# MLP up projection of a transformer block in seven half-size products in place of eight, for six of its eight chunks

## The reference, cut to what matters

```python
D_MODEL = 1024; SEQ = 1024; D_FF = 4 * D_MODEL     # one layer, batch 1, float32

def squared_relu_mlp(h, w1, w2):
    a = jax.nn.relu(h @ w1)
    return (a * a) @ w2
...
        x = x + g1 * (mix_lat @ w_out[i])
        x = x + g2 * squared_relu_mlp(modulate(x, g_mlp[i], sh2, sc2), w_mlp1[i], w_mlp2[i])
```

## Time and profile before

| | |
|---|---|
| median of 3 runs | 1398.17 us (1398.11 to 1398.28) |
| profiled execution, span from first to last instruction | 1394.5 us (the page gives no other time of that execution) |
| PE busy | 1351.0 us, 97% |
| DVE / ACT / POOL busy | 66% / 50% / 35% |
| MLP part of the span | about 730 us to the end |
| granted PE clock, mean | 0.994 |
| DMA | 143.42 MB, mean 103 GB/s |

### The profile page before, as it was taken

One profiled execution on the slowest core, in us unless ns is written; L12 is line 12 of the kernel. 1 busy time (PEld: TensorE's weight loads), 2 busy tenths in 40 slices (PEclk: granted clock), 3 DMA queues, 4 the chain that ended last, 5 costly groups with the idle time before them and its releaser, 6 DMA issues.

```text
span 1394.5 us, 18825 instructions
## 1 busy us (share of the span) xinstructions
PE 1351.0 (97%) x7262; PEld 1144.5 (82%) x7262; DVE 914.7 (66%) x1284; ACT 692.6 (50%) x1343; POOL 487.0 (35%) x321
## 2 busy tenths in 40 slices
...
GB/s 376 189 172 161 173 159 290 125 90 86 128 197 141 183 131 192 71 1 61 37 71 121 32 30 91 31 76 31 69 40 27 91 31 76 31 64 44 15 61 121
DMA packets 121576, 143.42 MB, mean 103 GB/s; under 512 B 8184, under 2 KB 103288, under 8 KB 118672
## 3 DMA queue, kind: packets, MB, share of 16 engines
q1 hardware_dynamic: 121232, 142.18, 32.3%
...
q0 software_dynamic: 256, 0.05, 0.0%
...
## 4 chain that ended last, share of the span: by engine, by line
PE 77%; DVE 12%; ACT 6%; DMA 2%; issue 1%; POOL 1%; SPq 0%; DVEq 0%; ACTq 0%
PE f_ps L2065 24%; PE f_ps L2334 19%; PE a_ps L1425 7%; PE o_ps L1773 6%; PE a_ps L1441 5%; PE a_ps L1471 5%; PE f_ps L2350 3%; ACT s_pr L1522 3%; DVE s_nmx L1607 2%; PE t_ps L956 2%; DMA t_wm<-in_w_mod 1%; PE t_ps L945 1%; PE t_ps L971 1%; ACT l_pr L1539 1%; DVE l_nb L1612 1%
## 5 line engine op out<-in xcount | busy, mean ns | idle before, releaser
L2065 PE MATMUL f_ps<-h,f_w 128*128 128x512 f32 x1536 | 358.0, 389 | 0.4 <-DVE h L1839 0.3
L2065 PEld LDWEIGHTS f_ps<-h,f_w 128*128 128x128 f32 x1536 | 288.2, 188 | 60.6 <-DVE h L1839 0.7
L2264 DVE TENSOR_TENSOR mix<-mix,f_ps 128x512 f32<-128x512 f32 x196 | 128.8, 684 | 152.8 <-PE f_ps L2334 152.8
L2105 POOL TENSOR_TENSOR f_w<-f_w,f_g 128x1024 f32<-128x1024 f32 x30 | 77.1, 2592 | 389.9 <-DMA f_w<-in_w_mlp 342.5
L2142 ACT ACTIVATE f_a<-f_ps 128x512 f32<-128x512 f32 x64 | 38.2, 597 | 255.0 <-PE f_ps L2065 254.9
L2334 PE MATMUL f_ps<-f_bl,f_ah 128*128 128x512 f32 x392 | 152.6, 389 | 0.0
L2334 PE MATMUL f_ps<-f_bh,f_ah 128*128 128x512 f32 x392 | 152.6, 389 | 0.0
L2334 PE MATMUL f_ps<-f_bh,f_al 128*128 128x512 f32 x392 | 152.5, 389 | 0.0
L1621 DVE TENSOR_TENSOR l_pT<-a_ps,l_pT 128x512 fp32r<-128x512 f32 (+1 forms) x192 | 109.0, 594 | 53.0 <-ACT l_pT L1532 53.0
L1425 PE MATMUL a_ps<-l_k,l_q 96*128 96x512 f32 (+1 forms) x576 | 136.4, 366 | 0.5 <-DVE l_mo L1633 0.5
L956 PE MATMUL t_ps<-w_in,t_h 128*128 128x416 f32 (+2 forms) x600 | 123.4, 351 | 0.3 <-DVE w_in L719 0.3
...
## 6 DMA issues: line engine op xcount, KB each, us to landing
...
f_w1r<-in_w_mlp SPq DMA_DIRECT2D x32, 512.0 KB, 4.1
f_w<-in_w_mlp SPq DMA_DIRECT2D x16, 1024.0 KB, 5.0
t_wm<-in_w_mod SPq DMA_DIRECT2D x8, 1024.0 KB, 12.6
...
```

What stands on the lines that cost most here:

```text
L2065: last = nc.tensor.matmul(ps[:, b, :], w1[:, g % 2, w, k, :], h2[x][:, k, half * HB:(half + 1) * HB], start=(k == 0 and i == 0), stop=(k = ...
L2264: V.tensor_tensor(x, x, ps[:, bank_of(i, t), :].rearrange("p (k c) -> p k c", c=P), ALU.add).then_inc(added, 1)
```

## The change

In chunks 2 to 7 the up projection too is made of seven half-size products, P5, P3, P2, P1, P6, P7, P4 in this order. h is cut in four quarters (token half `th`, half `kh` of the 1024 inputs), the chunk's part of w1 likewise ("11" to "22": input half, half of the 512 columns). Each product is 2 hidden tiles x 4 k x 3 = 24 matmuls of 512 tokens: 7 x 24 = 168 a chunk where there were 192. The results are chained in PSUM and through `a`: P5, P3 and P2 are copied out by ACT (`copy`), P1, P6 and P7 are added by DVE onto such a copy (`add`), ReLU and square follow (`square`).

- P2, P1 and P4 take quarters of `h2` as they are. P5, P3, P6 and P7 need four sums of quarters of h. They are made once, in two halves each, on VectorE (`sum_raw`: 20 instructions; `sum_low`: 8; high copies by ACT: 8), during chunks 0 and 1, stored to DRAM (`store_sum`, 16 DMAs of 512 KB), and read back in every chunk in 16 pieces of 512 KB into a ring of six places (`load_piece`).
- The differences of quarters of w1 are made on VectorE in each chunk (`mix_quads`, 4 a chunk); ACT and DVE split seven operands a chunk (`quad_high`, `quad_low`) where they split four. w1 comes as four quarters of 512 KB (`load_quad`).
- Chunks 0 and 1 keep the old up projection, but each `load_w1` now has stores in front of it or behind it. The sum that is stored is overwritten by the one after next only after its store has landed (`s_stored`).
- `h2` moves by 768 words, 3072 words are added for the sums and the ring, and the scratch space of software DMA is smaller.

```diff
+    def load_piece(c, j, k):
+        n = piece(c, j, k)
+        if n >= RING:
+            before = n - RING
...
+                sp.wait_ge(piece_used, USED0 + 12 * (bc_ - C0) + 3 * STREAM[bj] + bk + 1)
...
+    def sum_raw(half, j):
+
+        x = part[SUM_AT[j]][:, :, :]
...
+        if j == P5:
+            if half:
+                dve.wait_ge(s_stored, LOAD0 + 32 * sum_no(0, P3))
+            V.tensor_tensor(x, rows(0, 1, 0), rows(0, 1, 1), ALU.add).then_inc(s_made, 1)
+            dve.wait_ge(s_made, at - 2)
+            V.tensor_tensor(x, x, rows(1, 1, 0), ALU.add).then_inc(s_made, 1)
+            dve.wait_ge(s_made, at - 1)
+            V.tensor_tensor(x, x, rows(1, 1, 1), ALU.add).then_inc(s_made, 1)
+        if j == P6:
+            if half:
+                dve.wait_ge(s_stored, LOAD0 + 32 * sum_no(0, P7))
...
+        if j == P3:
+            dve.wait_ge(s_stored, LOAD0 + 32 * sum_no(half, P5))
...
+        if j == P7:
+            dve.wait_ge(s_stored, LOAD0 + 32 * sum_no(half, P6))
...
+    def sum_high(half, j):
+
+        act.wait_ge(s_made, MADE0 + RAW[half, j])
+        if (half, j) != SUMS[0]:
+            act.wait_ge(s_stored, LOAD0 + 32 * (sum_no(half, j) - 1))
+        nc.scalar.activation(parth[1][:, :, :], part[SUM_AT[j]][:, :, :], ACT.Copy).then_inc(s_hi, 1)
...
@@ sync
-        for g in range(2, 6):
-            load_w1(g)
-        for c in range(1, NCH):
-            load_w1(FC * c + 2)
-            load_w1(FC * c + 3)
-            if c < NCH - 1:
-                load_w1(FC * c + 4)
+        load_w1(2)
+        load_w1(3)
+        store_sum(0, P5)
+        load_w1(4)
+        store_sum(0, P6)
+        load_w1(5)
+        store_sum(0, P3)
+        store_sum(0, P7)
+        store_sum(1, P5)
+        store_sum(1, P6)
+        load_w1(6)
+        store_sum(1, P3)
+        load_w1(7)
+        store_sum(1, P7)
...
+            if c < LAST:
+                load_piece(c + 1, P5, 0)
+                load_piece(c + 1, P5, 1)
             load_w2(c, 0)
-            if c < NCH - 1:
-                load_w1(FC * c + 5)
+            if c < LAST:
+                load_quad(c + 1, "11")
+                load_quad(c + 1, "22")
+                for j, k in ((P5, 2), (P5, 3), (P3, 0), (P3, 1)):
+                    load_piece(c + 1, j, k)
             load_w2(c, 1)
@@ vector
+        sum_raw(0, P5)
+        sum_raw(0, P6)
+        sum_low(0, P5)
         w1_low(2)
+        sum_raw(0, P3)
+        sum_low(0, P6)
         w1_low(3)
+        sum_raw(0, P7)
+        sum_low(0, P3)
         w1_low(4)
+        sum_raw(1, P5)
+        sum_low(0, P7)
         low(0, M1)
-        for c in range(1, NCH):
+        sum_raw(1, P6)
+        sum_low(1, P5)
+        low(0, M2)
+        w1_low(5)
+        row_sums(0)
+        take(0, M1, 0, 1, 2, 3)
+        sum_raw(1, P3)
+        low(0, M6)
+        sum_low(1, P6)
+        take(0, M2, 0, 1)
+        w1_low(6)
+        take(0, M2, 2, 3)
+        sum_raw(1, P7)
+        sum_low(1, P3)
+        low(0, M5)
...
+        for c in range(C0, NCH):
             d = c - 1
...
             low(d, M7)
...
+            add(c, P7)
             take(d, M3, 2, 3)
             low(d, M4)
+            if c < LAST:
+                mix_quads(c + 1, 1)
             take(d, M7, 0, 1, 2, 3)
             if c < LAST:
+                quad_low(c + 1, P5)
+                mix_quads(c + 1, 2)
                 low(c, M1)
+                quad_low(c + 1, P3)
                 take(d, M4, 0, 1, 2, 3)
@@ tensor
+        for c in range(C0, NCH):
             d = c - 1
-            up_next(c, 0)
-            pe.wait_ge(rect, 8 * c)
+            up_streamed(c, P5)
             product(d, M1, 0, 1, 2, 3)
-            up_next(c, 1)
+            up_streamed(c, P3)
             product(d, M2, 0, 1)
-            up_next(c, 2)
+            up_kept(c, P2, 0)
             product(d, M2, 2, 3)
             product(d, M6, 0, 1, 2, 3)
```

More of the change, by code:

```diff
@@ L1930, in mlp_phase @@
     g2 = Z.room("tail", D)("f_g2", [P, D])
+    HK = KC // 2
     w1r = Z.room("R")("f_w1r", [P, KC, P])
+    far = Z.room("X", 2 * D)
+    wr = [room("f_wr%d" % i, [P, HK, 2 * P]) for i, room in enumerate((Z.room("R"), Z.room("tail", 2 * D), far))]
+    ring = Z.room("X")("f_ring", [P, 2, 2, BANK], F32R)
+    hq = Z.room("h2")("f_hq", [P, 2, KC, SEQ], F32R)
+    quarter = [hq[:, :, k, BANK:SEQ] for k in range(HK)] + [ring[:, i, :, :] for i in range(2)]
+    part = [Z.room("X", i * D)(f"f_part{i}", [P, 2, BANK]) for i in range(3)]
+    parth = [Z.room("X", i * D)(f"f_parth{i}", [P, 2, BANK], F32R) for i in range(3)]
     fin = Z.room("h2", KC * SEQ)("f_fin", [P, 2 * NB, HB])
@@ L2144, in rectify, with copy, square @@
             nc.scalar.activation(x, x, ACT.Square).then_inc(a_ready, 1)
+        def copy(c, j, f):
+            act.wait_ge(up_ready, unit(c, j, f))
+            if j == P5 and f == 0:
+                act.wait_ge(a_low, 7 * (c - 1))
+            nc.scalar.activation(block(c, j, f), ps[:, UPB[0] + f, :], ACT.Copy).then_inc(up_copied, 1)
+        def square(c, j):
+            n0 = 8 * c + 2 * (P1, P6, P7, P4).index(j)
+            for f in range(2):
+                x = block(c, j, f)
+                if j == P4:
+                    act.wait_ge(up_ready, unit(c, j, f))
+                    nc.scalar.activation(x, ps[:, UPB[0] + f, :], ACT.Relu).then_inc(rect, 1)
+                else:
+                    act.wait_ge(up_added, added_no(c, j, f))
+                    nc.scalar.activation(x, x, ACT.Relu).then_inc(rect, 1)
+                act.wait_ge(rect, n0 + f + 1)
+                nc.scalar.activation(x, x, ACT.Square).then_inc(a_ready, 1)
         def high(d, i):
@@ L2265, in take, with add @@
                 written[row, half] = n + 1
+        def add(c, j):
+            for f in range(2):
+                dve.wait_ge(up_ready, unit(c, j, f))
+                dve.wait_ge(up_copied, copied_no(c, {P1: P2, P6: P3, P7: P5}[j], f))
+                x = block(c, j, f)
+                V.tensor_tensor(x, x, ps[:, UPB[0] + f, :], ALU.add).then_inc(up_added, 1)
+        sum_raw(0, P5)
+        sum_raw(0, P6)
+        sum_low(0, P5)
         w1_low(2)
+        sum_raw(0, P3)
+        sum_low(0, P6)
         w1_low(3)
+        sum_raw(0, P7)
+        sum_low(0, P3)
         w1_low(4)
+        sum_raw(1, P5)
+        sum_low(0, P7)
         low(0, M1)
-        for c in range(1, NCH):
+        sum_raw(1, P6)
[13 more added lines that the diff above has]
+        low(0, M5)
+        take(0, M6, 0, 1, 2, 3)
+        difference(0, M3)
+        low(0, M3)
+        take(0, M5, 0, 1)
+        w1_low(7)
+        sum_low(1, P7)
+        take(0, M3, 0, 1)
+        take(0, M5, 2, 3)
+        difference(0, M7)
+        low(0, M7)
+        take(0, M3, 2, 3)
+        low(0, M4)
+        mix_quads(C0, 1)
+        take(0, M7, 0, 1, 2, 3)
+        quad_low(C0, P5)
+        mix_quads(C0, 2)
+        low(1, M1)
+        quad_low(C0, P3)
+        take(0, M4, 0, 1, 2, 3)
+        for c in range(C0, NCH):
             d = c - 1
             low(d, M2)
-            w1_low(FC * c + 1)
             row_sums(d)
+            quad_low(c, P2)
             take(d, M1, 0, 1, 2, 3)
```

321 lines of the change are left out of this document (275 added, 46 removed).

## The result

| | before | changed |
|---|---|---|
| median of 4 runs beside each other | 1398.20 us (1398.11 to 1398.28) | 1410.24 us (1407.16 to 1412.73) |
| ratio, 95% interval | | 1.0086 [1.0071, 1.0102] |
| profiled execution: own time, span | span 1394.5 us | 1411.49 us, span 1409.7 us |
| granted PE clock, mean | 0.994 | 0.979 |

The changed kernel is 0.86% slower. The forecast was 1407.6 us, slower by 0.7%.

What follows compares the result with a forecast made beforehand. PE was taken to bound the kernel: span 1394.5 - 32.6 (matmuls) + 31 (chunks 0 and 1) + 11 (chunk ends) = 1403.9 us, plus 3.7 to the median, 1407.6 us. The 8-in-10 range was 1381 to 1421.

Steps and rivals of the forecast that it cites:

- The gain: Chunks 2 to 7: 24 of 360 matmuls fewer in each of six chunks, 32.6 us less, a chunk becoming 76.2 us.
- Late place 1: Chunks 0 and 1: DVE's sums and their waits on stores make PE 31 us late by M5; bounds 20 and 36.
- The turns through DMA: Chunks 0 and 1: a w1 load with two stores behind it takes 6.9 us before DVE's next sums.
- POOL against DVE: All-SBUF instructions of the two engines alternate; each DVE instruction meeting a POOL one waits it out, 2.3 us.
- Late place 2: End of each chunk from 2 on: M4's and M2's takes late, 2.2 us at five boundaries, 11 us; bounds 1.5 and 20.
- The clock: PE after long waits in chunks 0 and 1: 0 to 1.7 us lost, nothing added; with every wait paying, 1414.
- The offset: Whole kernel: the median lies 3.7 us above the span of the profiled execution, so 3.7 us is added.
- PE-bound throughout: Whole kernel: 12 us lost in chunks 0 and 1, 0.3 at each boundary, giving 1379, faster; chance 0.2.
- Gain and loss cancelling: Chunks 0 and 1 lose 24 us, chunk ends 4: 1394 to 1400, say 1397; chance 0.2.
- Boundaries with a cooling PE: Five chunk boundaries cost 4.0 us of waits plus 1.7 of lower clock each, 28 us, giving 1425; chance 0.12.
- The starved ring: Ring of h pieces: transfers taking 3 us each in place of 1.4 cost 10 us more, giving 1418; chance 0.05.
- DVE's total: A chunk with the new up projection: DVE's 45.6 us plus 12.6 makes 58 of 76 us, not the bound.

Runs made afterwards that it cites:

- small gates: Changed kernel, with POOL's gates of w2's second half in chunks 2 to 6 multiplying 8 columns per tile in place of 1024: 1398.22 us.
- the kernel without sums: Changed kernel with the sums of h left out, quarters of h2 stored as they are in 16 same-size stores by SP: 1378.5 us.
- gates held: POOL's two gates of w2's second half wait for P3's split of the next chunk: 1420.96 us on the changed kernel, 1398.54 on the spread version.
- takes early: M4's takes moved ahead: 1418.98 us on the changed kernel; on the spread version, with two ring pieces moved ahead of a load on SP, 1400.17 us.
- spread version: Changed kernel with each w1_low ahead of store-waiting sums, sums spread over chunk 1, loads ahead of unrelated stores, POOL's first gates after w1_low(2): 1387.71 us.
- gates by DVE: On the spread version, DVE in place of POOL makes the two gates of w2's second half in chunks 2 to 6, behind M4's takes: 1388.13 us.

## Why the prediction was right, step by step

- **The gain, 32.6 us: right.** PE's blocks of 24 take 5.44 us as before, and the distance is 76.16 us where nothing waits (small gates, 912.68 to 988.84). 81.60 - 76.16 is 24 matmuls.
- **Late place 1, 31 us: right in place and cause; 34.4 in the profiled execution, 31.7 by the medians with and without the sums.** With 1.64 us taken off, `w1_low(2)` ended at 760.2 us (forecast 761.0), `w1_low(3)` at 772.2 (772.8), `w1_low(4)` at 785.6 (785.8), M1's splits at 801.9 (800.1), M5's at 847.0 (845.7). The first wait was 5.55 us in place of 6.7, the second none in place of 0.8, the third 1.26 in place of 2.1, M1's 10.42 in place of 8.8. (Forecast 0.7 for `w1_low(5)`: no wait.) The 3.4 us by which this execution exceeds the 31 are two terms: 1.3 us by which M5's splits came later, and 1.9 us of clock (below), which I had set to nothing. The turns through DMA, counted as in the forecast from the end of `w1_low` to DVE's next sum, were put at 6.9 us each and measured 7.3, 7.4 and 9.1. About 1.0 us of each is SP issuing the three DMAs one after the other (from 761.88 to 762.92 us in the first), which I had put at nothing. The long one, with P3's stores, is 2.2 us longer than forecast and by itself makes M1's splits late. The excess of the first two was made up for by `w1_low(2)`, which came 0.8 us early: a sum beside a gate took 3.3 us and not the 3.5 of my layout.
- **POOL against DVE: right.** "Each DVE instruction meeting a POOL instruction waits it out": four sums at 3.3 us, four gates at 13.24. The Trainium skill, "SBUF — State Buffer", section "SBUF: two separate sides", calls the port pair shared by the two an exclusive lock, held for a whole instruction; the alternation at 3.3 us agrees. Delaying the gates gave back 5.2 us by the medians.
- **Late place 2, 11 us: the cause right, the sum of 11.8 us partly luck.** I took the middle of 0.3 and 4.0 because the landing of w2's second half lay on the edge. It did: the first two boundaries cost 0.8 and 1.0 us, the last three 3.3. Neither end had the forecast size. With both gates among M1's splits, M4's takes were 1.53 us late (forecast 2.6) and M2's 0.63 (forecast 1.4). With the gates later they met M2's splits, which I had not looked at, and cost 0.8 in place of 0.3. That the errors cancel over two boundaries of one kind and three of the other is luck.
- **The clock: nothing added, 1.9 us measured.** The stretches of PE behind its waits (columns as in the earlier trace rows):

```profile
759.00:763.00 4.00, 1.09 (x3) 0.90 (x4) 2.86 (x3) 0.00 (x0) 0.00 (x0) 0.63 0.01 3
763.00:767.00 4.00, 4.00 (x11) 3.12 (x10) 0.00 (x0) 0.00 (x0) 0.00 (x0) 0.52 0.88 278
...
847.00:851.00 4.00, 2.29 (x6) 1.83 (x7) 4.00 (x7) 0.00 (x0) 0.00 (x0) 0.72 0.93 298
```

  After the wait of 5.55 us the clock is at half (1.2 of 2.4 GHz): 11 matmuls in 4 us where 17.6 fit, and the next wait is shorter for it, as forecast. Nothing swallows the last one: M5's first 12 matmuls took 4.58 us in place of 2.72. The rule of the Trainium skill ("TensorE: Matmul & The Clock Gate", section "Part 1: The HAM clock gate"), that idleness brings the lower clock, agrees with these rows. The sum of 1414 with every wait paying was too high, as the swallowed ones cost nothing.
- **The offset, 3.7 us: right.** It carries the sum from one fast execution's span to the median of before: 1.8 us is what lies between a span and its time wherever both are known, and the rest is how fast that execution was. So the forecast is 1398.2 - 32.6 + 31 + 11. With the losses of the profiled execution, 34.4 and 11.8, the same sum gives 1411.8; the median of the changed kernel is 1410.2, as that execution was slower than the median.
- **The rivals.** PE-bound throughout (1379): the kernel without sums ran at 1378.5, but the agreement is chance. That rival had 12 us lost in chunks 0 and 1 and 1.5 at the boundaries; the kernel without sums loses nothing in the first and the full 12 at the second. Gain and loss cancelling (1397) had 24 and 4 us; another order of stores gave 1396.5 with about 19 and 14. Boundaries with a cooling PE did not come in the changed kernel: the granted clock stayed 1.00 through the stretches around the boundaries before chunks 5 to 7. But the mechanism is real: it came in the edits that had single waits of 2.1 to 2.5 us there (gates held, on either version; takes early on the spread version; gates by DVE), behind most of them, and cost about 1.6 us a time. The starved ring did not occur here; it appeared when P3's split was made late.
- **DVE's total, 58 us a chunk: too small.** It is 67.9 of 79.4 us, and 76% of the span where I had about 70. Six DVE instructions of a chunk meet POOL's and take 3.4 us in place of 1.22, 13 us in all. The 58 had 3.4 us of such time from the kernel before, and no more was added. With the late gates small (62.4 us) it is 7.5 us.

What stays open: I found no order that mends the chunk ends, and cannot say that there is none; and the spread version's wait of 3.33 us in chunk 1 was not tried away. Whether shorter waits, kept apart so that the clock stays up, would turn the edits at the chunk ends into gains is open too.
